# Block matrices for the first product of each level in a recurrence's triangular inverse, and its systems grouped by head half

## What is computed

```python
def step(state, inp):
    r_t, w_t, k_t, v_t, kk_t, a_t = inp
    sa = jnp.einsum('bhij,bhj->bhi', state, -kk_t)
    state = (state * w_t[:, :, None, :]
             + sa[..., :, None] * (kk_t * a_t)[..., None, :]
             + v_t[..., :, None] * k_t[..., None, :])
    return state, jnp.einsum('bhij,bhj->bhi', state, r_t)

_, out = lax.scan(step, jnp.zeros((b, h, n, n), jnp.float32), xs)
```

## Time and profile before

| | |
|---|---|
| median of 3 runs | 2220.13 us |
| profiled execution, span | 2214.8 us |
| median less the span (what lies around it) | 5.3 us |
| PE busy / weight loads busy | 95% / 66% of the span |
| DVE / ACT / GpSimd busy | 54% / 35% / 1% |
| granted clock of TensorE, mean | 0.987 of 2.4 GHz |
| DMA, mean | 283 GB/s; 430 GB/s from 300 to 1160 us |

### The profile page before, as it was taken

The page is one execution under the profiler, slowest core; times in us unless marked ns, Lnnn a source line. Parts: engine busy times, 40 slices in busy tenths (PEclk is TensorE's granted clock), DMA queues, the critical chain, the costliest instruction groups (busy, mean ns, idle before and its releaser), DMA issues. The chain is left out here.

```text
span 2214.8 us, 34331 instructions
## 1 busy us (share of the span) xinstructions
PE 2114.3 (95%) x14251; PEld 1462.8 (66%) x14251; DVE 1195.3 (54%) x1882; ACT 766.2 (35%) x1011; POOL 16.9 (1%) x18
## 2 busy tenths in 40 slices
PE   7988999999998999999999999999999999999999
PEld 5767744333334433334437888988888888988888
DVE  5774513322222222223327876888765874888874
ACT  3553301111011100011105554556544553656543
POOL 0000000000000000000000000000000000000000
PEclk9999999999999999999999999999999999999999
DMA  9544699999999999999996555444655655444652
GB/s 373 185 165 198 258 416 430 428 431 430 431 429 430 429 430 430 428 430 431 430 427 215 191 194 167 155 147 147 199 191 186 194 190 190 152 136 133 209 191 76
DMA packets 200264, 625.87 MB, mean 283 GB/s; under 512 B 13200, under 2 KB 150352, under 8 KB 164304
## 3 DMA queue, kind: packets, MB, share of 16 engines
q1 hardware_dynamic: 197536, 622.41, 72.4%
q10 hardware_dynamic: 2608, 1.72, 0.3%
HBM read 623.05 MB, written 1.05 MB: 282 GB/s over the span
## 5 line engine op out<-in xcount | busy, mean ns | idle before, releaser
L2259 DVE TENSOR_TENSOR w_low<-ring,w_high 128x2048 fp32r<-128x2048 f32 x168 | 386.6, 2306 | 164.3 <-ACT w_high L2254 164.3
L2254 ACT ACTIVATE w_high<-ring 128x2048 fp32r<-128x2048 f32 x168 | 320.3, 1910 | 172.7 <-PE bank L2608 139.8
L2603 PE MATMUL bank<-h_both,w_high 128*128 128x512 f32 x1344 | 322.5, 392 | 0.0
L1965 PE MATMUL bank<-ring,ut 128*64 128x512 f32 x1024 | 249.3, 640 | 35.4 <-DMA ring<-in_exp_w_dram 35.4
L2603 PEld LDWEIGHTS bank<-h_both,w_high 128*128 128x128 f32 x1344 | 246.6, 188 | 48.9
L2054 ACT ACTIVATE sg<-glu 128x512 f32<-128x512 f32 x32 | 20.2, 630 | 567.6 <-DVE glu L2127 567.6
L1932 PE MATMUL bank<-ring_odd,xt 128*64 128x512 f32 x960 | 209.7, 594 | 2.9 <-DVE lin L2130 2.3
L1932 PE MATMUL bank<-ring,xt 128*64 128x512 f32 x960 | 209.3, 594 | 0.0
L1965 PEld LDWEIGHTS bank<-ring,ut 128*64 128x64 f32 x1024 | 74.2, 147 | 194.6 <-issue 132.3
L2143 DVE SCALAR_TENSOR_TENSOR xT<-bank,mod,xT 128x256 f32<-128x256 f32 x128 | 54.2, 477 | 224.4 <-PE bank L1976 224.4
L2608 PEld LDWEIGHTS bank<-h_both,w_low 128*128 128x128 f32 x1344 | 167.4, 188 | 7.0
(11 more groups left out here) (571 smaller groups left out, 2779.8 us busy)
## 6 DMA issues: line engine op xcount, KB each, us to landing
ring<-in_exp_w_dram SPq DMA_DIRECT2D x64, 2048.0 KB, 27.7
ring_odd<-in_exp_w_dram SPq DMA_DIRECT2D x64, 2048.0 KB, 27.8
ring<-in_exp_w_dram SPq DMA_DIRECT2D x128, 1024.0 KB, 25.4
ring<-in_ffn_w_gate_dram SPq DMA_DIRECT2D x44, 1024.0 KB, 5.2
ring<-in_ffn_w_up_dram SPq DMA_DIRECT2D x44, 1024.0 KB, 5.2
ring<-in_ffn_w_down_dram SPq DMA_DIRECT2D x44, 1024.0 KB, 4.9
ring<-in_w_in_dram SPq DMA_DIRECT2D x36, 1024.0 KB, 5.2
ring<-in_ada_w_dram SPq DMA_DIRECT2D x24, 1024.0 KB, 9.8
```

Of the source, the lines that this page charges most:

```text
L1965: ins = nc.tensor.matmul(bank[first + dh][at:at + 64, :], ut[:, r % 4, rows:rows + 64], w[:, x, 512 * dh:512 * dh + 512], start=False, sto ...
L2254: nc.scalar.activation(w_bufs[0][u % BUFS], ring2[:, u % RING2, :], ACT.Copy).then_inc(high2, 1)
L2259: nc.vector.tensor_tensor(w_bufs[1][u % BUFS], ring2[:, u % RING2, :], w_bufs[0][u % BUFS].bitcast(F32), ALU.subtract).then_inc(low2, 1)
L2603: return nc.tensor.matmul(b[:, :], w_parts[0][:, at:at + P], moving.rearrange("p a t -> p (a t)"), start=start, stop=False, skip_group_che ...
```

## The change

x_product becomes one matmul per system: its weights are a 128x128 matrix, `low_blocks[:, s_, :]`, whose two blocks hold the two chunks' triangles (on the diagonal for one group, off it for the other, with zeros elsewhere), and it streams `inv_t[:, s_, :]` over all 128 rows. The block matrices lie in `states`; GpSimd clears their zero quarters, and ACT fills the others by four copies of 64 rows. The groups are now the systems 0 to 7 and 8 to 15, that is, by `h2`. Two calls of `clear` move from level 4 to behind the loop. growth_t and growth keep their matmuls.

```diff
-            @S.block.gpsimd
-            def _(gps):
-                S.clear_former(gps)
-
-            low, inv, inv_t, xs = (x.rearrange("p (s t) -> p s t", t=CH) for x in ring_scratch[4:8])
+            inv, inv_t, xs = (x.rearrange("p (s t) -> p s t", t=CH) for x in ring_scratch[5:8])
...
+            low_blocks = states[:, :, :, :].rearrange("p c h t -> p (c h) t")
...
             def inverse_rows(s_, ph):
-                return half_rows(ph if s_ % 2 else 1 - ph)
+                return half_rows(ph if s_ >= NS // 2 else 1 - ph)
 
             def group(x, g):
-                return x[:, g:NS:2, :]
+                return x[:, NS // 2 * g:NS // 2 * g + NS // 2, :]
...
+            @S.block.gpsimd
+            def _(gps):
+                S.clear_former(gps)
+                for g in range(2):
+                    for ph in range(2):
+                        nc.gpsimd.memset(group(low_blocks, g)[half_rows(ph), :, half_rows(ph if g == 0 else 1 - ph)], 0.0).then_inc(S.sem("low_cleared"), 1)
...
                 def place(b, rows, s_):
-                    return bank[b][rows, CH * (s_ // 2):CH * (s_ // 2) + CH]
-
-                def x_product(s_, ph):
-                    return nc.tensor.matmul(place(4 + s_ % 2, inverse_rows(s_, ph), s_), low[half_rows(ph), s_, :], inv_t[half_rows(ph), s_, :],
-                                            start=True, stop=True)
+                    return bank[b][rows, CH * (s_ % (NS // 2)):CH * (s_ % (NS // 2)) + CH]
+
+                def x_product(s_):
+                    return nc.tensor.matmul(place(4 + s_ // (NS // 2), slice(0, P), s_), low_blocks[:, s_, :], inv_t[:, s_, :], start=True, stop=True)
...
                     else:
                         pe.wait_ge(sem("inv_t_set"), 4)
-                        pe.wait_ge(sem("low_ready"), 2)
+                        pe.wait_ge(sem("low_cleared"), 4)
+                        pe.wait_ge(sem("low_ready"), 2 * g + 2)
...
-                for s_ in range(0, NS, 2):
-                    for ph in range(2):
-                        ins = x_product(s_, ph)
+                for s_ in range(NS // 2):
+                    ins = x_product(s_)
                 ins.then_inc(sem("x_ready0"), 1)
                 for n in range(LEVELS):
                     wait_x(n, 1)
                     wait_growth_t(n, 0)
-                    for s_ in range(0, NS, 2):
+                    for s_ in range(NS // 2):
                         for ph in range(2):
                             grown = growth_t(s_, ph)
-                        for ph in range(2):
-                            ins = x_product(s_ + 1, ph)
+                        ins = x_product(NS // 2 + s_)
...
                 act.wait_ge(sem("low_product"), 1)
-                for h2 in range(2):
-                    st.tell(nc.scalar.activation(flat(low[:, 8 * h2:8 * h2 + 8, :]), bank[4 + h2][:, :], ACT.Copy), "low_ready")
+                for g in range(2):
+                    for ph in range(2):
+                        st.tell(nc.scalar.activation(group(low_blocks, g)[half_rows(ph), :, half_rows(1 - ph if g == 0 else ph)],
+                                                     bank[4 + g][half_rows(ph), :].rearrange("p (s t) -> p s t", t=CH), ACT.Copy), "low_ready")
                 for n in range(LEVELS):
                     for g in range(2):
                         act.wait_ge(sem(f"x_ready{g}"), n + 1)
                         st.tell(nc.scalar.activation(group(xs, g), bank[4 + g][:, :].rearrange("p (s t) -> p s t", t=CH), ACT.Copy), f"x_taken{g}")
-                        if n:
+                        if 1 <= n <= 3:
                             clear(2 * (n - 1) + g)
...
-                for k in range(2 * (LEVELS - 1), 12):
+                for k in range(6, 12):
                     clear(k)
```

More of the change, by code:

```diff
@@ L1137, in place @@
                 def place(b, rows, s_):
-                    return bank[b][rows, CH * (s_ // 2):CH * (s_ // 2) + CH]
-                def x_product(s_, ph):
-                    return nc.tensor.matmul(place(4 + s_ % 2, inverse_rows(s_, ph), s_), low[half_rows(ph), s_, :], inv_t[half_rows(ph), s_, :],
-                                            start=True, stop=True)
+                    return bank[b][rows, CH * (s_ % (NS // 2)):CH * (s_ % (NS // 2)) + CH]
+                def x_product(s_):
+                    return nc.tensor.matmul(place(4 + s_ // (NS // 2), slice(0, P), s_), low_blocks[:, s_, :], inv_t[:, s_, :], start=True, stop=True)
                 def growth_t(s_, ph):
                     r = inverse_rows(s_, ph)
-                    return nc.tensor.matmul(place(2 + s_ % 2, half_rows(ph), s_), inv[r, s_, :], xs[r, s_, :], start=True, stop=True)
+                    return nc.tensor.matmul(place(2 + s_ // (NS // 2), half_rows(ph), s_), inv[r, s_, :], xs[r, s_, :], start=True, stop=True)
                 def wait_x(n, g):
@@ L1166, in growth @@
                         pe.wait_ge(sem("products_taken"), 2)
-                    for s_ in range(g, NS, 2):
+                    for s_ in range(NS // 2 * g, NS // 2 * g + NS // 2):
                         for ph in range(2):
@@ L1221, in _ @@
                         wait_x(n + 1, 0)
-                    for s_ in range(0, NS, 2):
+                    for s_ in range(NS // 2):
                         for ph in range(2):
-                            grown = growth_t(s_ + 1, ph)
+                            grown = growth_t(NS // 2 + s_, ph)
                         if n + 1 < LEVELS:
-                            for ph in range(2):
-                                ins = x_product(s_, ph)
+                            ins = x_product(s_)
                     grown.then_inc(sem("growth_t1"), 1)
```

## The result

The changed kernel takes 2273.49 us (median; 2272.24 to 2278.29) against 2219.51 (2218.72 to 2220.39) for the kernel before on the same chip: 1.0248 times as long, with an interval of 1.0233 to 1.0262. That is 54 us more, where 30 were forecast with a range that ended at 42. The profiled execution took 2273.9 us, its span 2272.1.

The account below looks back on a forecast made before the run. Instruction fetch was taken to pace the inverse. First x block to 156.6, mixed blocks 45.4, growths and kappa 9.3, rest 2.9 end it at 214.2 against 184.09: 2220.1 + 30.1 = 2250 us, range 2236 to 2262.

Parts of the forecast that it names:

- What bounded the kernel: Inverse paced by instruction fetch, 3.5 us per 128 load-matmul pairs; any delay there passes one for one to the end.
- The first x block: First x_product block of the inverse, full-array alone: 0.16 + 14 x 0.112 = 1.7 us to its last start; growth_t at 156.6.
- The change of shape: Mixed growth_t/x_product blocks: switching 64x64 tiles to full array costs 0.15 us, back 0.20; a system 0.63 against 0.12.
- Rival A: Mixed blocks: quadrant and full matmuls follow without a pause, 0.34 us a system; +9, 2229 us; 12%.
- rival B: Mixed blocks: no drain, full loads hide behind growth_t, fetch keeps the pace; 2215.8 us; 4%.
- The clock: Whole inverse priced at full clock: nine mixed blocks at 5.04 us, ten growth and kappa products at 0.93.
- Rival C: Mixed blocks: granted clock falls because few columns are streamed; up to 36 us more, 2286 us; 6%.
- the allowance of 1.5 us: Behind the inverse: fetch pauses move to other instructions as pages shift by 160 pairs; 1.5 us either way.
- all of 5.3 us: Runs' median 2220.13 lies 5.3 us above the profiled span 2214.8; taken as left alone by the change.
- The hidden edits: Memsets, four copies, moved clears and new grouping, on engines beside PE: cost nothing while their cover stands.

Follow-up runs that it names:

- e6: Kernel before, leaving out the x products of seven of the eight systems in each of nine mixed blocks (126 matmuls): 2213.32 us, 0.9977.
- e7: Kernel before with growth_t for all eight systems of a mixed block, then their x_products, on two quadrants at a time: 2218.53 us, 0.9997.
- e1: Changed kernel with each mixed block's eight growth_t first, then its eight full x_products (2 shape changes, not 16): 2226.23 us, 1.0035.
- e2: Changed kernel alternating growth_t and x_product by four systems (4 shape changes a block), 2230.53 us, and by two (8 changes), 2237.42 us.
- e5: Changed kernel with x_product streaming 128 columns instead of 64, still 16 shape changes a block: 2248.72 us, 1.0137.
- e4: Changed kernel with all its other edits, but x_product again as two 64x64 matmuls a system: 2218.41 us, 0.9998.

## Why the prediction was right and where it failed

**What bounded the kernel: right.** e6 and e7 bear out both halves of it. Fewer pairs made the inverse 4.8 us shorter, and array work slower by 8 us made it 1.7 longer. The delay passed nearly one for one, 58.9 us at SP's wait and 57.3 at the end.

**The first x block: right.** 153.70 with 16 records, growth_t at 156.58 against a forecast of 156.6. The 0.112 us a record from L1310 held. The rule of the Trainium skill (TensorE: Matmul & The Clock Gate, Part 3, The mechanism), by which a load overlaps matmuls in flight only where the row group differs, would make every gap here 0.16 us, 2.4 for the 15 between these 16 records. They took 1.7 (2.00 less the last one's 0.28), and the measurement decides.

**The change of shape: right.** 0.63 us a system was forecast and 0.63 measured; e1 and e2 give about 0.145 us a change, against 0.15 from the earlier trace rows. The Trainium skill (TensorEngine Tiling (Array Packing), Tiling Modes) says that changing the mode drains the engine, and the trace agrees, with this number and the loader's 7.6 us of idle time beside it. Rival A (no drain) and rival B (faster) fall with it.

**The clock: wrong, and it is the step that failed.** The sum priced all of the inverse at full clock, 9 x 5.04 for the mixed blocks and 10 x 0.93 for growth and kappa. The trace has a granted clock of 0.50 for 71.7 us of it, where a block takes 8.2 and a growth 1.76. Rival C, which says so, had 6%, against it "no idle time over 0.2 us, and L1310's records, loads for the greater part too, keep their pace to the end". Neither held as a reason. The clock fell at 159.0 and at 176.0 with PE busy on either side. An idle 0.89 us, the wait for ACT's copy, ends 2.4 us before the first fall, but the kernel before, e1 and e5 have the same wait and keep the clock; ahead of the second fall, PE was busy for all of 10.2 us. And L1310's run lasts 3.8 us, while the mixed blocks go on for 45: it could not speak for them. "Streams columns a third of the time at most" was in the text, as the argument for, and e5 bears it out.

What it cost, from the rows: 6.8 + 64.9 = 71.7 us were spent at half clock. A block with its growth takes 8.2 + 1.8 = 10.0 us there for 5.04 + 0.93 = 6.0, so that work would have taken 0.6 of it at full clock, 43 us. That puts 29 us on the clock and leaves 29 of the 58.3 for the changes of shape and the loads, where the forecast had 30.1. e5 gives the same split by a run: +32.7, with 0.05 us more in each of its 9 x 7 wide systems, 3 us, so +29.5 for the narrow form.

C's own price, 2286, was too high by 12 us. About 4 of these lie outside the inverse, which grew by 58.3 where the time grew by 54 (next paragraph). Inside, three things work against each other: a system slows by 1.64 at half clock and not by the 1.8 of C's price, the growths, which C left out, slow by 1.9, and some 13 us of the inverse's work behind 156.6 ran at full clock. Why a system slows by less than 2 isn't shown.

**Around the span.** The pauses behind the inverse moved as the allowance of 1.5 us had it: one of 1.54 us went, another grew by 0.6, 1.0 us less in all. The measured +54 is smaller than the span's +57.3 for another reason: the profiled execution of before was itself a quick one. Around the span of after lie 1.8 us (2273.9 less 2272.1); if as much lies around that of before, its profiled execution took some 2216.6 by this estimate, where its runs have a median of 2219.5. The forecast took all of 5.3 us as lying around the span.

**The hidden edits: right.** e4 puts memsets, copies, clears and grouping at nothing.

**Why the other order didn't save it.** e1 is the best form with full-array products found here, and still 0.35% slower than before. A block of 3.0 us is eight full products at 2 x 0.112 = 1.8 and growth_t at 1.1: the two no longer lie beside each other. By fetch the old block's 64 pairs are 1.75 us, and nine blocks at 1.25 more are 11.3, about the 11.2 measured. By this reckoning the loads of full weights cost more than the 160 pairs that they save.

**What stays open.** What exactly brings the clock down isn't settled. The change and e5 show that streaming more columns in the same pattern keeps it up. But columns streamed per us don't put all the kernels in order: a block with 4 changes streams its 3072 columns in 3.24 us, e5 its 3968 in 5.4, and the one with fewer per us, e5, is the one whose trace has no fall. Nor is it settled what brings the clock back. All four returns (165.8 and 240.9 in the changed kernel, 164.4 with 8 changes, 164.8 with 4) come in work on 64x64 tiles alone, growth, kappa or the last growth_t, but the growth and kappa product at 177.7 to 181.2 in the changed kernel brought none. The runs don't show which quantity is watched. No kernel here beats the one before with its whole work done; e6's 0.23% is what leaving products out gives.

## What to carry to other kernels

Keep one shape of tile for a run of matmuls: each change between quadrants and the full array costs about 0.145 us, more than the 0.112 of a full-array record, and at 16 a block it was more than the products themselves. Where small matmuls pause at a fixed count of instructions, array packing is worth next to nothing (1.7 us of the inverse here, none of the time) and fewer instructions are worth the fetch rate alone; price the replacement's loads before trading four small records for two big ones. And PE can lose the clock with no idle time at all, for whole blocks and the products between them: look at the columns streamed too, and not only at the idle column of the profile, before taking full clock for granted.

## What the runs showed of the hardware that was not expected

- The granted clock fell to 0.50 for 64.9 us in a stretch where PE shows no idle time, and stayed at 1.00 when the same pattern streamed 128 columns for 64 (e5). More streamed work made the kernel 25 us faster.
- With 4 and with 8 changes a block the clock fell for 6.8 us at nearly the same place (158.0 and 157.6), came back in the growth and kappa product behind that block, and stayed up in the mixed blocks that followed. In the changed kernel it came back too, for 10 us, and fell again.
- At half clock, six records with two changes of shape between them slow by 1.64, not by 2: 0.63 to 1.03 us. A growth slows by 1.9, 0.93 to 1.76.
- Twice the columns (128 for 64) on a full-array fp32 product cost 0.05 us a pair of records (0.68 for 0.63 a system).
- Losing the overlap of all four quadrants in nine blocks (e7) changed the time by nothing that can be measured (0.9997).
